# Folded inverses, post-norms behind the maxima, and output halves copied before they are squared, in a hybrid attention layer

## The chip, the cores and the metric

The kernel runs on one core of one Trainium2 chip. The metric is the device time of one execution in microseconds, taken as the median of several runs.

TensorE (PE in the profile) multiplies matrices into PSUM, VectorE (DVE), ScalarE (ACT) and GpSimd (POOL) work on rows of elements, and SyncE (SP) issues transfers. PEld is the loading of a matmul's weights.

## The reference

One layer of a streaming encoder, for a prompt of 2048 frames and for 32 new frames of a running stream with 1024 old ones:

```python
h = rmsnorm(x, g_pre)
u_a, gate_a, q, k, v, qi, ki, wi, gate_b = split(h @ w_in)
y_a = pool_mixer(u_a)                      # trailing means, a linear map per group
score = einsum(wi, relu(qi @ ki))          # 8 index heads of 32; only visible chunks of 64
sel = top_k(score, 256)                    # per query
logits = q @ k[sel] * HEAD_DIM**-0.5 + rel_bias[bucket(sel - pos)]   # 8 heads of 64, 2 kv heads
y_b = softmax(logits) @ v[sel]
mixed = concat([y_a * silu(gate_a), y_b * silu(gate_b)])
y = x + rmsnorm(mixed @ w_out, g_post)
```

## The kernel before

The queries are cut into 17 tiles: 16 of 128 prompt frames and one with the 32 new frames, tile 16. A first phase (not touched) projects, makes the pool branch and the index scores and leaves q, gates and scores in DRAM. The second phase, function `phase2`, runs through steps t = -1 to 19. A softmax over the selected keys is done as a softmax over all visible keys plus a mask of -1e30 on those that were not selected.

In step t, side by side:

- TensorE makes for each job (kv head, key tile) of tile t the logits (four matmuls, lines 1613 to 1618: high and low part of q, mask, and the row maximum taken away, "shift"), and two jobs later the weighted values (L1633, which sum the softmax's denominators in the same product). In between come the logits of tile t+1 that only serve its row maxima (L1599) and the output product of tile t-2 (L1648), in two halves of 512 columns with eight matmuls each, both into the one PSUM bank `wide[1][:, 0:512]`. A tile t below 16 has 2(t+1) jobs.
- ScalarE exponentiates each job into one of four buffers `E` (L1576), copies sums and denominators out of PSUM (L1515, L1517), takes the two output halves (kind "Y": square with an accumulated sum, L1564, then copy into `osb`, L1568), and makes the first 16 rounds of the search for the 256th score of tile t+3 (L1542 and small steps).
- VectorE makes rounds 16 to 25 of the search of tile t+2 (kind "R", L345 to L352) and its mask ("C", `set_mask`, L370 to L1693), the maxima of tile t+1 ("M", L1711), from them the shift ("S", L1716 and eight times L1721), the inverses of the denominators of tile t-1 ("I", L1727), and the post-norm of tile t-3 ("P", `post_norm`: a root by three Newton rounds on one column each, then L1736).
- GpSimd multiplies the exponentials of the six nearest key tiles of each kv head with the position bias (L1501), multiplies the sums of tile t-1 with the inverses and the gate (`mean`, L1460 and L1466, the result `yT` feeds the output product), and adds the residual to tile t-3 (`residual`, L1473).
- SP issues the loads of the next tiles and the store of tile t-3, in the order of its program; where it waits, all that is behind it waits.

The order on each engine is written out by `in_order`, which gives each kind of work a first and a last place within the step, between 0 and 1, and sorts. VectorE's today:

```python
return in_order((rounds, 0.0, 0.8), ([("M", *m) for m in maxima_of(t + 1)], 0.08, 0.78),
                ([("I", t - 1)] if 0 <= t - 1 < NT else [], 0.2, 0.2),
                ([("P", t - 3)] if 0 <= t - 3 < NT else [], 0.5, 0.5),
                ([("S", t + 1)] if 0 <= t + 1 < NT else [], 0.79, 0.79),
                ([("C", u)] if searched(u) else [], 0.9, 0.9))
```

Three PSUM banks hold the maxima's logits in turn, two hold the jobs' logits. Tiles from `FIRST` = 6 on are searched in phase 2. `NT` is 17, `ST` is 16, `NKV` 2, `HD` 64, `GRP` 4 and `P` 128.

Of the kernel before, what the change touches and what calls it, by code (L numbers as in the profile page):

```python
# [16 lines left out]
ALU = mybir.AluOpType  # L17
# [218 lines left out]
def build(nc, A):  # L236
    ctx = ExitStack()
    with ctx:
# [8 lines left out]
        def dram(name, shape, dt=F32):  # L247
# [10 lines left out]
        k_dram = dram("sample_keys_scratch", (NKV, P, PAST + P))  # L258

# [19 lines left out]
               ma_dram, s_dram, m_dram, g_dram, k_dram)  # L279
        phase2(nc, A, sb, sem, identf, identb, onesb, k2, home, loaded, unit, xs, first_q, banks, wide, q_dram, gb_dram,  # L280
               ma_dram, s_dram, m_dram, g_dram, k_dram)
# [127 lines left out]
def phase1(nc, A, sb, sem, identf, identb, onesb, k2, home, loaded, unit, xs, first_q, banks, wide, q_dram, gb_dram, ma_dram,  # L409
           s_dram, m_dram, g_dram, k_dram):  # L410
# [806 lines left out]
def phase2(nc, A, sb, sem, identf, identb, onesb, k2, home, loaded, unit, xs, first_q, banks, wide, q_dram, gb_dram, ma_dram,  # L1217
           s_dram, m_dram, g_dram, k_dram):
# [41 lines left out]
    HALVED = 1 + 3 * ZOOM_AT  # L1260

# [21 lines left out]

    def dve_step(t):
        u = t + 2
        rounds = [("R", u, r) for r in range(ZOOM_AT, ALL_ROUNDS)] if searched(u) else []
        return in_order((rounds, 0.0, 0.8), ([("M", *m) for m in maxima_of(t + 1)], 0.08, 0.78),
                        ([("I", t - 1)] if 0 <= t - 1 < NT else [], 0.2, 0.2),
                        ([("P", t - 3)] if 0 <= t - 3 < NT else [], 0.5, 0.5),
                        ([("S", t + 1)] if 0 <= t + 1 < NT else [], 0.79, 0.79),  # L1290
                        ([("C", u)] if searched(u) else [], 0.9, 0.9))

    def act_step(t):
        u = t + 3
        pieces = []
        if searched(u):
            pieces = [("N", u)]
            for r in range(ZOOM_AT):
                pieces += [("K", u, r), ("T", u, r)]
        return in_order(([("E", *j) for j in jobs(t)], 0.0, 1.0), (pieces, 0.02, 0.96),  # L1300
                        ([("Y", t - 2, 0)] if 0 <= t - 2 < NT else [], 0.5, 0.5),
                        ([("Y", t - 2, 1)] if 0 <= t - 2 < NT else [], 1.0, 1.0))

    with ExitStack() as st:
# [9 lines left out]

        act_junk = sb(st, "act_junk", [P, SEQ], BF16)
# [13 lines left out]
        sq = sb(st, "sq", [P, 512], BF16)  # L1329
        mxp = sb(st, "mxp", [P, NH, 4], F32)  # L1330
        nmax = sb(st, "nmax", [P, NH], F32)
        ss2 = sb(st, "ss2", [P, NT, 2], F32)
# [28 lines left out]
        sums_out, recip_done = sem("sums_out"), sem("recip_done")  # L1361
        mean_done, yT_done = sem("mean_done"), sem("yT_done")
        o_full, o_free = sem("o_full"), sem("o_free")
# [3 lines left out]
        with nc.Block() as block:  # L1367
            @block.sync
            def _(sp):
# [29 lines left out]

                def load_out_weights(i):  # L1400
# [3 lines left out]
                for t in range(NT + 3):  # L1404
# [20 lines left out]
                    if t + 4 >= FIRST + 3:  # L1425
                        load_S(t + 4)
                    if t >= 3:
# [26 lines left out]
            def _(pool):  # L1454
                def mean(t):

                    pool.wait_ge(recip_done, t + 1)
# [29 lines left out]
                for t in range(NT + 3):  # L1487
                    todo = jobs(t)
                    for i in range(len(todo) + 1):
                        if i == len(todo) // 3 and 0 <= t - 1 < NT:  # L1490
                            mean(t - 1)
                        if i == 2 * len(todo) // 3:
                            if t - 3 >= 0:
                                residual(t - 3)
# [11 lines left out]
            def _(act):  # L1506
# [20 lines left out]
                for t in range(NT + 2):  # L1527
                    for kind, *at in act_step(t):
# [30 lines left out]
                        elif kind == "Y":  # L1559
                            b, i = at  # L1560
                            act.wait_ge(o_full, 2 * b + i + 1)
                            if 2 * b + i:
# [265 lines left out]
```

## Time and profile before

| | before |
|---|---|
| median of 3 runs | 1710.84 us (1708.82 to 1711.71) |
| profiled execution | 1709.82 us |
| its span, first to last instruction | 1708.0 us |
| busy TensorE, VectorE, ScalarE, GpSimd | 1571.0, 1212.5, 893.6, 473.1 us |
| mean granted TensorE clock | 0.966 |

Phase 2 begins at about 800 us. Step 6 begins at 979.8 us, step 12 at 1333.4, step 13 at 1408.3, step 14 at 1485.9, step 15 at 1562.4 and step 16 at 1637.3, each taken as the start of the first logits matmul of its tile. Busy times of matmuls overlap with their neighbours' and their ends are modelled, so starts are the better measure of TensorE's pace.

### The profile page before, as it was taken

What the parts mean: (1) busy time and instruction counts of PE and PEld (TensorE: products, weight loads), DVE (VectorE), ACT (ScalarE), POOL (GpSimd) and SP (SyncE); (2) the same over time, 40 slices, a digit from 0 to 9 for tenths busy, and PEclk for the clock granted to TensorE, in tenths of its full rate; (3) what the DMA queues carried; (4) which work ended last, traced back from release to release, by engine and by line L of the source; (5) the groups of instructions that cost most, each with busy time, mean ns of one, the idle gap of its engine ahead of it and who ended that gap; (6) DMA issues with size and microseconds to landing.
All of it is one profiled execution on the core that took longest, in us unless ns stands there. A gap on an engine that the chain in (4) does not pass through costs nothing.

```text
span 1708.0 us, 17799 instructions
## 1 busy us (share of the span) xinstructions
PE 1571.0 (92%) x5191; PEld 877.6 (51%) x5191; DVE 1212.5 (71%) x2940; ACT 893.6 (52%) x1684; POOL 473.1 (28%) x384
## 2 busy tenths in 40 slices
PE   7999899989998989887888988999999999899996
PEld 4555555555555867655444444444444444455552
DVE  5412555557767878875549999999998999985422
ACT  3112333344434334452299988998888786523331
POOL 0112111121112112111344443433433333322241
PEclk9999999989999989988899999999999999999999
DMA  9312322221111110047533222220230211201001
GB/s 360 73 39 49 95 52 53 63 70 60 51 52 49 41 59 32 35 149 199 163 93 102 63 67 56 82 84 25 60 87 25 51 33 30 62 11 39 31 32 49
DMA packets 91978, 120.76 MB, mean 71 GB/s; under 512 B 17149, under 2 KB 63805, under 8 KB 91498
## 3 DMA queue, kind: packets, MB, share of 16 engines
q1 hardware_dynamic: 90506, 115.44, 21.7%
q10 hardware_dynamic: 1376, 4.19, 2.1%
q8 instruction: 42, 0.69, 0.2%
q14 instruction: 54, 0.44, 0.1%
HBM read 76.06 MB, written 43.54 MB: 70 GB/s over the span
## 4 chain that ended last, share of the span: by engine, by line
PE 23%; DVE 17%; ACT 6%; issue 5%; POOL 2%; POOLq 0%; DVEq 0%; ACTq 0%
PE wide L1648 7%; PE wide L1633 7%; DVE above L345 6%; DVE max_junk L1711 3%; ACT act_junk L1542 2%; PE bank L1613 2%; PE bank L1614 2%; PE bank L1615 2%; PE bank L1618 2%; POOL E L1501 1%; PE bank L1599 1%; DVE den L1727 1%; ACT E L1576 1%; DVE reach L383 1%; DVE S L379 1%
## 5 line engine op out<-in xcount | busy, mean ns | idle before, releaser
L931 PE MATMUL bank<-hT,home 128*128 128x512 f32 (+2 forms) x1280 | 489.5, 523 | 4.6 <-ACT kq L831 2.0
L1501 POOL TENSOR_TENSOR E<-E,home 128x512 f32<-128x512 f32 (+1 forms) x174 | 251.9, 1451 | 446.6 <-ACT E L1576 446.5
L931 PEld LDWEIGHTS bank<-hT,home 128*128 128x128 f32 x1280 | 241.2, 195 | 173.3 <-issue 150.6
L1633 PE MATMUL wide<-E,home 128*128 128x512 f32 x544 | 284.8, 605 | 9.9 <-POOL E L1501 9.7
L1576 ACT ACTIVATE E<-bank 128x512 f32<-128x512 f32 (+1 forms) x290 | 165.5, 571 | 244.9 <-PE bank L1618 243.2
L907 ACT ACTIVATE relu<-wide 128x1024 f32<-128x1024 f32 (+7 forms) x192 | 153.3, 802 | 173.5 <-PE wide L949 98.9
L1183 DVE SCALAR_TENSOR_TENSOR S<-relu,wi,S 128x1024 f32<-128x1024 f32 (+7 forms) x168 | 175.1, 1042 | 78.6 <-ACT relu L907 68.9
L1711 DVE CUSTOM_DVE_ANT_0 max_junk<-bank,mask 128x512 bf16<-128x512 f32 (+3 forms) x230 | 136.9, 614 | 68.9 <-PE bank L1599 55.4
L1648 PE MATMUL wide<-home 128*128 128x512 f32 x272 | 142.3, 614 | 23.2 <-ACT osb L1568 23.0
L949 PE MATMUL wide<-kiT,qiT 96*128 96x512 f32 (+3 forms) x304 | 136.4, 520 | 23.5 <-ACT relu L907 23.4
L1542 ACT ACTIVATE act_junk<-S,minus_cand 128x1152 bf16<-128x1152 f32 (+5 forms) x105 | 155.4, 1480 | 1.4
L931 PE MATMUL bank<-home,hT 128*128 128x296 f32 (+1 forms) x544 | 146.7, 410 | 2.5 <-ACT hT L815 2.5
L1648 PE MATMUL wide<-home,yT 128*128 128x512 f32 x272 | 135.8, 593 | 0.0
L1633 PEld LDWEIGHTS wide<-E,home 128*128 128x128 f32 x544 | 104.0, 194 | 55.5 <-POOL E L1501 17.7
L931 PEld LDWEIGHTS bank<-home,hT 128*128 128x128 f32 x544 | 106.5, 198 | 31.4 <-issue 4.6
L345 DVE TENSOR_SCALAR_CACHE_REDUCE above<-S,search 128x1152 bf16<-128x1152 f32 (+5 forms) x70 | 118.6, 1694 | 0.5
L744 POOL TENSOR_TENSOR win<-U 128x512 f32<-128x512 f32 (+11 forms) x20 | 20.1, 1005 | 356.8 <-ACT U L851 356.8
L1615 PE MATMUL bank<-identb,mask 128*128 128x512 bf16 (+1 forms) x290 | 112.8, 389 | 0.0
L1613 PE MATMUL bank<-first_q,k 128*128 128x512 f32 x182 | 107.5, 591 | 4.7 <-issue 2.6
L1618 PE MATMUL bank<-shift,onesb 128*128 128x512 bf16 (+1 forms) x290 | 109.6, 378 | 0.0
L1599 PE MATMUL bank<-k,first_q 128*128 128x512 f32 (+3 forms) x145 | 92.0, 659 | 14.5 <-DVE mxp L1711 9.7
L1711 DVE CUSTOM_DVE_ANT_0 max_junk<-wide,mask 128x512 bf16<-128x512 f32 (+3 forms) x114 | 65.3, 573 | 38.9 <-PE wide L1599 21.4
(204 smaller groups left out, 2390.0 us busy)
## 6 DMA issues: line engine op xcount, KB each, us to landing
xs<-x_prompt SPq DMA_DIRECT2D x16, 512.0 KB, 4.1
home<-w_in SPq DMA_DIRECT2D x16, 512.0 KB, 13.2
xr<-x_prompt SPq DMA_DIRECT2D x16, 512.0 KB, 4.3
y_prompt<-osb SPq DMA_DIRECT2D x16, 512.0 KB, 2.9
first_q<-q_high_scratch SPq DMA_DIRECT2D x24, 256.0 KB, 5.1
s_scratch<-S SPq DMA_DIRECT2D x11, 512.0 KB, 2.7
first_q<-q_low_scratch SPq DMA_DIRECT2D x18, 256.0 KB, 4.1
gb<-gb_scratch SPq DMA_DIRECT2D x17, 256.0 KB, 5.4
```

The lines of the kernel that those rows point to most:

```text
L345: dve.tensor_scalar((B.above, B.reach)[i][:, 0:s.shape[1]], s, B.cand[:, i:i + 1], None, ALU.is_ge, ALU.add, accum_out=B.cnt[:, i:i + 1]). ...
L907: act.activation(relu[:, k % 2, 0:b - a], wide[k % 2][:, 0:b - a], ACT.Relu)\
L931: mm = pe.matmul(out, stationary(c), moving(c), start=(c == 0), stop=(c == DC - 1))
L1183: dve.scalar_tensor_tensor(row, relu[:, k % 2, 0:b - a], w, row, ALU.mult, ALU.add)\
L1501: pool.tensor_tensor(E[:, k % 4, :, 0:n], E[:, k % 4, :, 0:n], EB[:, kv * GRP:(kv + 1) * GRP, off:off + n], ALU.mult)\
L1542: act.activation(act_junk[:, 0:w], S[sslot(u)][:, 0:w], ACT.Sign, bias=minus_cand[:, u % 2:u % 2 + 1], accum_out=act_sum[:])\
L1576: act.activation(E[:, k % 4, :, 0:n], banks[2 + k % 2][:, 0:GRP * n].rearrange("p (j n) -> p j n", j=GRP), ACT.Exp).then_inc(fl_free, 1)
L1615: pe.matmul(bank, mask[:, t % 3, kt * P:(kt + 1) * P], identb[:, 0:n].rearrange("p (a n) -> p a n", a=1).broadcast_to([P, GRP, n]), start= ...
L1618: pe.matmul(bank, onesb[:], shift[:, t % 2, kv * GRP:(kv + 1) * GRP, 0:n], start=False, stop=True)\
L1633: pe.matmul(wide[0][:, kv * 512:kv * 512 + GRP * n].rearrange("p (j n) -> p j n", j=GRP), values[:, kt, kv:kv + 2, :].rearrange("p a d -> ...
L1648: mm = pe.matmul(wide[1][:, 0:512], stat, wout[:, c, i * 512:(i + 1) * 512], start=(c == 0), stop=(c == DC - 1))
L1711: dve.tensor_tensor_reduce(junk[:, k % 2, 0:b - a], max_banks[k % 3][:, 0:b - a], mask[:, t % 3, a:b], 1.0, LEAST, ALU.add, ALU.max, mxp[: ...
```

## The change

Three things change. First, for tiles 5 to 14 (`FOLDED`) the denominators, 512 values in each of two partitions (copies in 64 partitions each), are folded by two transfers into 8 values on each of 128 partitions, inverted there, and brought back through DRAM with two broadcasting transfers; GpSimd's `mean` waits for these. VectorE's inverse moves from 0.2 to 0.4 of a step, `mean` from one third to two thirds of the jobs. Second, the post-norm moves behind the shift, from 0.5 to 0.80, in steps 6 to 15 (`long`), and the residual on GpSimd to the end of the step's jobs. Third, ScalarE only copies each output half (at 0.46 and 0.96 of the step), and squares both halves from `osb` in one instruction at 0.06 of the following step; TensorE waits for one count a half instead of two. Beside these, the shift of 8 heads is one VectorE instruction with broadcast operands.

```diff
+        r_dram = dram("reciprocal_scratch", (2, NKV, 1, GRP * P))
...
+    FOLDED = range(FIRST - 1, NPT - 1)
...
+    def long(t):
+
+        return FIRST <= t < ST
+
     def dve_step(t):
...
-                        ([("I", t - 1)] if 0 <= t - 1 < NT else [], 0.2, 0.2),
-                        ([("P", t - 3)] if 0 <= t - 3 < NT else [], 0.5, 0.5),
                         ([("S", t + 1)] if 0 <= t + 1 < NT else [], 0.79, 0.79),
+                        ([("I", t - 1)] if 0 <= t - 1 < NT else [], *((0.4, 0.4) if t - 1 in FOLDED else (0.2, 0.2))),
+                        ([("P", t - 3)] if 0 <= t - 3 < NT else [], *((0.80, 0.80) if long(t) else (0.5, 0.5))),
                         ([("C", u)] if searched(u) else [], 0.9, 0.9))
...
-                        ([("Y", t - 2, 0)] if 0 <= t - 2 < NT else [], 0.5, 0.5),
-                        ([("Y", t - 2, 1)] if 0 <= t - 2 < NT else [], 1.0, 1.0))
+                        ([("Y", t - 2, 0)] if 0 <= t - 2 < NT else [], 0.46, 0.46),
+                        ([("Y", t - 2, 1)] if 0 <= t - 2 < NT else [], 0.96, 0.96),
+                        ([("Z", t - 3)] if 0 <= t - 3 < NT else [], 0.06, 0.06))
...
+                def fold(t):
+
+                    i, turn = t % 2, t - FOLDED[0]
+                    sp.wait_ge(sums_out, 4 * (t + 1))
+                    for kv in range(NKV):
+                        sp.dma_start(folded[kv * HD:(kv + 1) * HD, i],
+                                     den[kv * HD:kv * HD + 1, i].rearrange("p (a n) -> p a n", a=HD))\
+                          .then_inc(folded_in[i], 16)
+                    sp.wait_ge(recip_done, t + 1)
+                    sp.dma_start(r_dram[i].rearrange("k o (a n) -> (k o a) n", a=HD), folded[:, i]).then_inc(folded_out, 16)
+                    sp.wait_ge(folded_out, 16 * (turn + 1))
+                    for kv in range(NKV):
+                        sp.dma_start(den[kv * HD:(kv + 1) * HD, i], r_dram[i, kv].broadcast_to([HD, GRP * P]))\
+                          .then_inc(spread_in, 16)
...
                     if t + 4 >= FIRST + 3:
                         load_S(t + 4)
+                    if t - 1 in FOLDED:
+                        fold(t - 1)
...
-                    pool.wait_ge(recip_done, t + 1)
+                    if t in FOLDED:
+                        pool.wait_ge(spread_in, 32 * (t - FOLDED[0] + 1))
+                    else:
+                        pool.wait_ge(recip_done, t + 1)
...
-                        if i == len(todo) // 3 and 0 <= t - 1 < NT:
+                        if i == (2 if t - 1 in FOLDED else 1) * len(todo) // 3 and 0 <= t - 1 < NT:
                             mean(t - 1)
-                        if i == 2 * len(todo) // 3:
-                            if t - 3 >= 0:
-                                residual(t - 3)
+                        if i == (len(todo) if long(t) else 2 * len(todo) // 3) and t - 3 >= 0:
+                            residual(t - 3)
...
-                            if 2 * b + i:
-                                act.wait_ge(o_free, 4 * b + 2 * i)
-                            act.activation(sq[:], wide[1][:, 0:512], ACT.Square,
-                                           accum_out=ss2[:, b, i:i + 1]).then_inc(o_free, 1)
                             if i == 0 and b >= 2:
                                 act.wait_ge(y_out[b % 2], 16 * (b // 2))
                             act.activation(osb[:, b % 2, i * 512:(i + 1) * 512], wide[1][:, 0:512], ACT.Copy).then_inc(o_free, 1)
+                        elif kind == "Z":
+                            b = at[0]
+                            act.wait_ge(o_free, 2 * b + 2)
+                            act.activation(sq[:], osb[:, b % 2], ACT.Square, accum_out=ss2[:, b:b + 1])\
+                               .then_inc(squared, 1)
...
-                    if c == 0 and 4 * t + 2 * i:
-                        pe.wait_ge(o_free, 4 * t + 2 * i)
+                    if c == 0 and 2 * t + i:
+                        pe.wait_ge(o_free, 2 * t + i)
...
-                    for h in range(NH):
-                        ins = dve.tensor_scalar(shift[:, t % 2, h, :], identb[:], nmax[:, h:h + 1], None, ALU.mult)
-                    ins.then_inc(shift_done, 1)
+                    dve.tensor_tensor(shift[:, t % 2], identb[:].rearrange("p (a n) -> p a n", a=1).broadcast_to([P, NH, P]),
+                                      nmax[:].rearrange("p (h n) -> p h n", n=1).broadcast_to([P, NH, P]), ALU.mult)\
+                       .then_inc(shift_done, 1)
 
                 def invert_sums(t):
+                    if t in FOLDED:
+                        dve.wait_ge(folded_in[t % 2], 32 * (1 + (t - FOLDED[0]) // 2))
+                        dve.reciprocal(folded[:, t % 2], folded[:, t % 2]).then_inc(recip_done, 1)
+                        return
...
-                    dve.wait_ge(o_free, 4 * (t + 1))
-                    link(dve.tensor_tensor(root[:, 3:4], ss2[:, t, 0:1], ss2[:, t, 1:2], ALU.add))
-                    dve.wait_ge(dk, n)
-                    n = inverse_root(dve, dk, n, root[:, 0:1], root[:, 1:2], root[:, 2:3], root[:, 3:4], 1.0 / D)
+                    dve.wait_ge(squared, t + 1)
+                    n = inverse_root(dve, dk, n, root[:, 0:1], root[:, 1:2], root[:, 2:3], ss2[:, t:t + 1], 1.0 / D)
```

## Rows read from the trace of the kernel before

**Rows 1.** Windows: length; busy PE, PEld, DVE, ACT, POOL (instructions); clock; DMA.

```profile
979.80:1485.90 506.10, 467.93 (x1475) 230.60 (x1473) 482.09 (x1038) 418.69 (x776) 192.66 (x120) 0.99 0.19 54
...
1333.40:1408.30 74.90, 68.54 (x223) 33.67 (x221) 72.02 (x143) 61.86 (x105) 26.63 (x16) 1.00 0.16 44
1562.40:1637.30 74.90, 74.90 (x249) 38.02 (x248) 21.84 (x71) 23.59 (x43) 20.41 (x16) 1.00 0.13 36
...
1395.20:1420.50 25.30, 22.67 (x72) 10.55 (x71) 24.78 (x33) 19.72 (x36) 14.20 (x6) 1.00 0.27 62
...
1347.20:1395.20 48.00, 45.47 (x152) 23.26 (x152) 45.64 (x111) 38.65 (x66) 12.54 (x9) 1.00 0.06 23
```

**Rows 2.** Timeline of TensorE late in step 15: start, us, instruction.

```profile
1626.81 0.79 PE L1613 MATMUL bank<-first_q,k 128*128 128x512 f32 x1
...
1629.43 0.80 PE L1613 MATMUL bank<-first_q,k 128*128 128x512 f32 x1
...
1631.20 0.79 PE L1613 MATMUL bank<-first_q,k 128*128 128x512 f32 x1
```

**Rows 3.** TensorE's waits in steps 6 to 13: us in total, times, longest.

```profile
PE bank L1599 <- DVE mxp L1711: 16.5, 15, 2.6
PE wide L1633 <- POOL E L1501: 8.1, 8, 1.7
```

**Rows 4.** Groups of VectorE by form, steps 6 to 13: busy us, mean ns.

```profile
L1727 DVE RECIPROCAL den<-den 128x512 f32<-128x512 f32 x8 | 26.8, 3347 | 0.0
...
L1721 DVE TENSOR_SCALAR shift<-identb,nmax 128x128 bf16<-128x128 bf16 x64 | 18.1, 354 | 0.7 <-DVE nmax L1716 0.5
```

**Rows 5.** The tile of the denominators: shortest, median and longest reciprocal in ns.

```profile
L1727 DVE RECIPROCAL den<-den x17: 953/3348/3354, 816.1 to 1666.5; 128x512 f32<-128x512 f32 x16, 128x128 f32<-128x128 f32 x1
```

**Rows 6.** Timeline of VectorE, the post-norm in step 12.

```profile
1376.27 0.15 DVE L1732 TENSOR_TENSOR root<-ss 128x1 f32<-128x1 f32 x1
1376.46 0.15 DVE L286 TENSOR_SCALAR root<-root 128x1 f32<-128x1 f32 x1
...
1378.58 1.28 DVE L1736 SCALAR_TENSOR_TENSOR osb<-osb,root,gpost 128x1024 f32<-128x1024 f32 x1
```

**Rows 7.** Timeline of SP's queue in step 12.

```profile
1340.54 0.33 SPq L1376 DMA_DIRECT2D S<-s_scratch  x1
1382.41 0.34 SPq L1431 DMA_DIRECT2D y_prompt<-osb  x1
```

**Rows 8.** DMA issues of phase 2: count, KB each, median us to landing.

```profile
gb<-gb_scratch SPq DMA_DIRECT2D x16, 256.0 KB, 5.4
...
gpost<-g_post SPq DMA_DIRECT2D x1, 512.0 KB, 16.3
...
y_sample<-osb SPq DMA_DIRECT2D x1, 128.0 KB, 1.9
```

**Rows 9.** Timeline of VectorE, the post-norm in step 16.

```profile
1645.75 0.35 DVE L1732 TENSOR_TENSOR root<-ss 128x1 f32<-128x1 f32 x1
...
1647.57 1.20 DVE L296 SCALAR_TENSOR_TENSOR root<-root 128x1 f32<-128x1 f32 x1
...
1651.06 1.29 DVE L1736 SCALAR_TENSOR_TENSOR osb<-osb,root,gpost 128x1024 f32<-128x1024 f32 x1
```

**Rows 10.** Timelines of GpSimd and VectorE at the end of step 12.

```profile
1398.21 1.28 POOL L1501 TENSOR_TENSOR E<-E,home 128x512 f32<-128x512 f32 x1 [1.15 <-ACT E L1576]
1401.33 11.63 POOL L1501 TENSOR_TENSOR E<-E,home 128x512 f32<-128x512 f32 x4 [1.84 <-ACT E L1576]
...
1401.54 5.07 DVE L379 TENSOR_TENSOR_SCAN S<-reach,above 128x1920 f32<-128x1920 bf16 x1
```

**Rows 11.** Timeline of ScalarE, the last output half.

```profile
1698.40 0.60 ACT L1564 ACTIVATE sq<-wide 128x512 bf16<-128x512 f32 x1 [7.22 <-PE wide L1648]
...
1698.99 0.59 ACT L1568 ACTIVATE osb<-wide 128x512 f32<-128x512 f32 x1
```

**Rows 12.** TensorE's waits for output halves: steps 2 to 5, step 16 onwards.

```profile
PE wide L1648 <- ACT osb L1568: 12.7, 6, 3.3
...
PE wide L1648 <- ACT osb L1568: 5.0, 4, 1.4
```

More of the change, by code:

```diff
@@ L278, in build @@
         phase1(nc, A, sb, sem, identf, identb, onesb, k2, home, loaded, unit, xs, first_q, banks, wide, q_dram, gb_dram,
-               ma_dram, s_dram, m_dram, g_dram, k_dram)
+               ma_dram, s_dram, m_dram, g_dram, k_dram, r_dram)
         phase2(nc, A, sb, sem, identf, identb, onesb, k2, home, loaded, unit, xs, first_q, banks, wide, q_dram, gb_dram,
-               ma_dram, s_dram, m_dram, g_dram, k_dram)
+               ma_dram, s_dram, m_dram, g_dram, k_dram, r_dram)
 def inverse_root(dve, done, n, ms, y, tmp, ss, scale):
@@ L409, in phase1 @@
 def phase1(nc, A, sb, sem, identf, identb, onesb, k2, home, loaded, unit, xs, first_q, banks, wide, q_dram, gb_dram, ma_dram,
-           s_dram, m_dram, g_dram, k_dram):
+           s_dram, m_dram, g_dram, k_dram, r_dram):
     steps, inside = phase1_steps()
@@ L1217, in phase2 @@
 def phase2(nc, A, sb, sem, identf, identb, onesb, k2, home, loaded, unit, xs, first_q, banks, wide, q_dram, gb_dram, ma_dram,
-           s_dram, m_dram, g_dram, k_dram):
+           s_dram, m_dram, g_dram, k_dram, r_dram):
     def chunks(t):
@@ L1313, in phase2 @@
         mask = sb(st, "mask", [P, 3, SEQ], BF16)
+        sq = sb(st, "sq", [P, D], BF16)
         act_junk = sb(st, "act_junk", [P, SEQ], BF16)
@@ L1328, in phase2 @@
         yT = sb(st, "yT", [P, 2, 4, P], F32)
-        sq = sb(st, "sq", [P, 512], BF16)
+        folded = sb(st, "folded", [P, 2, NH], F32)
         mxp = sb(st, "mxp", [P, NH, 4], F32)
         nmax = sb(st, "nmax", [P, NH], F32)
-        ss2 = sb(st, "ss2", [P, NT, 2], F32)
+        ss2 = sb(st, "ss2", [P, NT], F32)
         root = sb(st, "root", [P, 4], F32)
@@ L1361, in phase2 @@
         sums_out, recip_done = sem("sums_out"), sem("recip_done")
+        folded_in = [sem(f"folded_in{i}") for i in range(2)]
+        folded_out, spread_in = sem("folded_out"), sem("spread_in")
         mean_done, yT_done = sem("mean_done"), sem("yT_done")
-        o_full, o_free = sem("o_full"), sem("o_free")
+        o_full, o_free, squared = sem("o_full"), sem("o_free"), sem("squared")
         post_done = sem("post_done")
@@ L1526, in _ @@
                 waiting = []
-                for t in range(NT + 2):
+                for t in range(NT + 3):
                     for kind, *at in act_step(t):
```

## Prediction

> **What bounds the kernel now.** I read the windows by step first. A step here is one turn t of phase 2's loop: logits, exponentials and weighted values of tile t, the maxima of tile t+1, the output product of tile t-2. Steps 6 to 13 took 506.1 us; VectorE was busy for 482.1 of them, TensorE for 468 [rows 1]. Both look full, so I asked next what TensorE would need alone. In step 15, where it waits for nothing, a job with an output product beside it takes 2.62 us from one first logits matmul to the next, a job alone 1.77 [rows 2]; so an output product is 0.85 and one 512-column pass about (1.77 - 0.85) / 4 = 0.23. Step 15 then needs 32 x 1.77 + 16 x 0.85 + 18 x 0.23 = 74.4 us against 74.9 measured [rows 1]: the reckoning holds. Steps 6 to 13 have 168 jobs, 128 output products and maxima worth 184 passes: 297.4 + 108.8 + 42.3 = 448.5 us. So they run 58 us above TensorE's own work and only 24 above VectorE's. The waits say the same: TensorE's longest is for the maxima's two banks, 16.5 us, the next for GpSimd's bias products, 8.1 [rows 3]. VectorE sets these eight steps; step 15 and most of step 14 belong to TensorE.
>
> VectorE's step has two halves. Between the last maximum of tile 13 and the first of tile 14 lie shift, mask and the first search rounds, 25.3 us without a maximum; TensorE was busy for 22.7 of them with work that needs no maxima. In the stretch of tile 13's maxima, 48.0 us, VectorE was busy for 45.6 [rows 1]. TensorE's own work there is some 42 us: the maxima go from 0.15 (three buffers filled) to 0.76 of its step, so 0.61 of 26 jobs, 9.5 output products and 25 passes. The second half is where VectorE holds the step up by itself.
>
> **Folded inverses.** Eight full reciprocals in steps 6 to 13 take 3.35 us each [rows 4]. The folded one has 8 elements a partition. The two shapes seen, 3348 ns for 512 and 953 for 128 [rows 5], give 6.24 ns an element and 0.20 us at 8. Bounds: 0.15, a one-column operation [rows 6], and 0.95. I take 0.20: 3.15 saved, 25.2 us over eight steps. In step 14 and 15 the saving falls where TensorE is full and counts nothing.
>
> The price is five transfers a tile on SP's queue: two fold, one goes out, two spread. Behind them on SP stand the store, the load of the residual's input and the next step's loads. Today SP stands from the score load at 1340.5 to the store at 1382.4 with nothing to do [rows 7], so the fold uses idle time. The fold's rows are issued behind the step's loads, 7 us into step 12 today [rows 7]; with the store before them pushed by some 10 us and landings of 5.4, they are there near 20, and the inverse is asked for later: VectorE begins step 12's maxima at 1347.2, 13.8 us in [rows 1], 0.18 of the step where 0.08 is written, so place 0.4 comes near 0.5, plus 3 us of post-norm: 27 us in a step 6 of 49.
>
> After it come the way out and the spread. Transfers land in 1.9 us at best, in a burst in 5.4, the slowest seen in 16.3 [rows 8]. I take 2 + 2.5 + 1 us of issuing, 5.5, because nothing else is queued then; bounds 4 and 33. GpSimd multiplies at two thirds of the jobs, in front of most of the second head group's bias products. In step 6 the mean is done at 27 + 5.5 + 2 x 1.28 = 35 us; the weighted values of the job behind it run two jobs late, at 11/14 of 49 = 38.5. So it costs nothing, and the room after the inverse is 38.5 - 27 - 2.6 = 9 us in step 6 and 62 - 38.5 - 2.6 = 21 in a step 12 of 71.
>
> **Shift in one instruction.** Eight small ones take 18.1 / 8 = 2.26 us a step; a two-source operation on 1024 elements takes 1.28 [rows 4, 6]. It can wait for one GpSimd product (1.28) first [rows 10]. Bounds 1.28 and 2.56; I take 1.7, the row and a third of such a wait: 0.56 saved, 4.5 us.
>
> **Post-norm after the shift.** The sum of the two halves goes (0.19, start to start [rows 6]): 1.5 us. The other 12 instructions stay, but the place changes. Today GpSimd stands idle waiting for exactly this chain, which takes 1376.27 to 1379.86, 3.59 us [rows 6]. In step 16, beside GpSimd's products, the same chain took 1645.75 to 1652.35, 6.60 us [rows 9]. The new place, 0.8 of a step, lies among the second group's bias products. Bounds: 0 and 3.0 us more a step; I take 1.0, nearer to the quiet row since the products leave gaps, so -8.0 us. The chain moves 3.4 us out of the maxima's stretch into the other half, which was level with TensorE; that half becomes longer, but VectorE's sum decides both.
>
> The Trainium skill (SBUF — State Buffer, section "SBUF: two separate sides") calls this an exclusive lock: a VectorE operation with two SBUF inputs and a GpSimd operation exclude each other for the whole instruction. The rows agree: GpSimd's four products of 1.28 took 11.63 us while VectorE ran the scan and the two-source operations behind it [rows 10]. Applied to every small operation of the chain, this rule would give the upper bound, 3.0 in place of 1.0, and 16 us less gain.
>
> In return the residual no longer stands on GpSimd in front of bias products, and the mask's operations slide past the step's last products. TensorE's waits there are 8.1 us [rows 3]; I take 3 of them. What is late next is the residual: it ends some 10 us into the following step and the store follows, before the copy at 0.46 wants that buffer.
>
> **Copy first, square later.** Square to copy, start to start, is 0.59 us [rows 11]; TensorE waits for the pair. Steps 2 to 5 have six such waits, 12.7 us, the end four, 5.0 us [rows 12]. In steps 2 to 5 I take 6 x 0.59 less a little for ScalarE, itself near full with the search: 3 us. The waits in steps 6 to 13 bring nothing while VectorE binds. At the end three waits in line save 1.8; the last square, now 1024 wide (estimate 1.2 from two of 0.6, and 0.2 to read the sum), stands after the copy and gives back 0.6: 1.2 us.
>
> **Sum.** 25.2 + 4.5 + 1.5 - 8.0 + 3 = 26.2 us in steps 6 to 13, 3 in 2 to 5, 1.2 at the end: 30.4. The profiled execution took 1709.8 us (1.8 around its span); 1679.4. The median of the runs is 1.0 above it: 1680.
>
> **Rivals.** *TensorE's pace.* If shorter VectorE stretches also end its own idle 24 us, steps 6 to 13 come near VectorE's 459 (TensorE's 448.5 lies below): 47 + 4 = 51 us off, 1660. For it: GpSimd's jam by the scan, in most steps, is the start of VectorE's idle; against: the two engines then stand within 3% and interleave in a fixed order. Chance 0.14.
>
> *The first half becomes the brake.* The post-norm lengthens the stretch without maxima to about 28 to 31 us while TensorE has 23 to 25 of work; the maxima's stretch can fall no further than TensorE's 42, 6.0 less than today. With a chain of 6.6 us a step gives up 6.0 (less the shift's 0.6) and gains 6.0 to 6.7: eight steps bring some 5, the rest 4: 1702. For it rows 9, against it that VectorE's own sum still falls. Chance 0.15.
>
> *The inverses come too late* (slower). GpSimd then stands in front of the second group's bias products, and TensorE's weighted values behind them. The room is 9 us in step 6 and about 2 more in each following step. A way out at the slowest landing and a spread at a burst's, 16.3 + 5.4 + 1 = 22.7 us, would cost 14, 12, 10 ... 2 us in steps 6 to 12, 56 in all: 1736. It outweighs the 30 from about 19 us on. Against: the quiet queue; the 16.3 comes from a full 512 KB broadcast to all partitions in the burst of step 1. Chance 0.10.
>
> *Nothing measurable:* the gains are what VectorE then spends waiting, 1711. Against: rows 3. Chance 0.05.
>
> **Numbers.** The forecast, own range 1665 to 1693, has 0.56. A measurement tells about 0.2% (3.4 us) from no change. Faster: 0.56 + 0.14 + 0.14 of the third case = 0.84; same 0.06; slower 0.10. To hold 8 in 10 the range takes in the forecast, most of the third case and two thirds of the first rival: 1657 to 1705.
>
> **What would show it.** Steps 6 to 13 at 475 to 485 us; a folded reciprocal near 0.2; one shift of 1.3 to 2.6; the chain of the post-norm at 3.4 to 6.4; TensorE's waits for maxima cut to a third, but moved to the first maxima of a step; GpSimd not waiting for the spread in front of bias products; waits for the copied halves down by 0.6 each. Wrong if VectorE's busy time falls by 25 us and the steps don't, or if GpSimd's wait for the spread shows up in TensorE.

## The result, and the profile after

| | before | after |
|---|---|---|
| median | 1710.84 us (5 runs, 1708.82 to 1714.02) | 1719.69 us (5 runs, 1718.05 to 1720.34) |
| ratio, 95% interval | | 1.0049 (1.0034 to 1.0063) |
| profiled execution, span | 1708.0 us | 1717.9 us |
| busy TensorE, VectorE | 1571.0, 1212.5 us | 1573.6, 1191.8 us |
| mean granted TensorE clock | 0.966 | 0.957 |

The changed kernel is slower by 0.5%, where 1.8% faster was forecast. Step 6 now begins at 975.8 us, step 12 at 1335.9, step 13 at 1413.8, step 14 at 1492.4, step 15 at 1574.4 and step 16 at 1649.5. The windows of the changed kernel, columns as in [rows 1]: steps 6 to 13, step 14, the stretch without maxima between tiles 13 and 14, and the stretch of tile 13's maxima:

```profile
975.80:1492.40 516.60, 470.43 (x1475) 237.55 (x1473) 465.76 (x967) 415.53 (x758) 192.37 (x119) 0.96 0.20 55
1492.40:1574.40 82.00, 76.40 (x247) 39.16 (x245) 65.23 (x138) 22.30 (x39) 26.45 (x15) 0.96 0.14 36
...
1402.40:1431.70 29.30, 24.34 (x77) 11.45 (x75) 28.39 (x39) 21.91 (x39) 15.31 (x7) 1.00 0.32 83
1354.40:1402.40 48.00, 47.24 (x152) 24.75 (x152) 39.81 (x98) 38.09 (x64) 10.26 (x8) 0.93 0.05 18
```

Against [rows 1], VectorE's busy time in steps 6 to 13 fell by 16.3 us (482.1 to 465.8), and these steps took 10.5 us more (506.1 to 516.6). The stretch without maxima grew from 25.3 to 29.3 us. The stretch of tile 13's maxima is 48.0 us as before, although VectorE has only 39.8 us of work in it instead of 45.6. What it saved there it now spends waiting; its waits in steps 6 to 13, of the changed kernel:

```profile
DVE max_junk L1741 <- PE bank L1629: 22.4, 25, 2.1
DVE max_junk L1741 <- PE wide L1629: 16.3, 16, 2.5
```

38.7 us, where VectorE had waited 11.4 us in the same places before:

```profile
DVE max_junk L1711 <- PE bank L1599: 7.8, 10, 2.1
DVE max_junk L1711 <- PE wide L1599: 3.6, 5, 1.5
```

And TensorE, same steps, to be set against [rows 3] (the matmul of the maxima is now L1629, VectorE's maximum L1741, the weighted values L1663):

```profile
PE bank L1629 <- DVE mxp L1741: 30.1, 6, 5.9
PE wide L1629 <- DVE mxp L1741: 9.3, 3, 8.3
PE wide L1663 <- POOL E L1530: 5.5, 4, 1.7
```

[rows 3] show the waits for the maxima's two banks only; the third buffer, a half of `wide[1]`, has a line of its own, before:

```profile
PE wide L1599 <- DVE mxp L1711: 7.8, 6, 2.7
```

So 21 waits of at most 2.7 us, 24.3 us in all, have become nine, 39.4 us in all. Seven of these nine are long (4.0 to 8.3 us), one a step from step 7 on. Each of the seven stands in front of the fourth matmul of a tile's maxima: three buffers are filled, and the first is not read yet. The longest, in TensorE's timeline of step 12:

```profile
1345.17 0.79 PE L1629 MATMUL bank<-k,first_q 128*128 128x512 f32 x1
1345.80 1.02 PE L1678 MATMUL wide<-home 128*128 128x512 f32 x2
...
1355.16 0.58 PE L1629 MATMUL wide<-k,first_q 128*128 128x256 f32 x1 [8.34 <-DVE mxp L1741]
```

What VectorE did meanwhile (its timeline: the shift, the post-norm from its first to its last instruction, the scan of the mask, the end of the second search round, the first maximum):

```profile
1326.50 1.23 DVE L1750 TENSOR_TENSOR shift<-identb,nmax 128x1024 bf16<-128x1024 bf16 x1
1327.64 0.15 DVE L287 TENSOR_SCALAR root<-ss 128x1 f32<-128x1 f32 x1
...
1329.49 1.14 DVE L297 SCALAR_TENSOR_TENSOR root<-root 128x1 f32<-128x1 f32 x1
...
1331.44 1.28 DVE L1768 SCALAR_TENSOR_TENSOR osb<-osb,root,gpost 128x1024 f32<-128x1024 f32 x1
...
1337.01 4.77 DVE L380 TENSOR_TENSOR_SCAN S<-reach,above 128x1792 f32<-128x1792 bf16 x1
...
1354.25 0.16 DVE L353 SCALAR_TENSOR_TENSOR search<-search,search 128x1 f32<-128x1 f32 x1
1354.40 0.69 DVE L1741 CUSTOM_DVE_ANT_0 max_junk<-wide,mask 128x512 bf16<-128x512 f32 x1
```

The post-norm took 5.08 us here (1327.64 to 1332.72), in front of mask and search and so in front of the first maximum. The last reading is the clock. A window around that stand:

```profile
1350.90:1361.10 10.20, 5.94 (x12) 3.07 (x13) 9.35 (x24) 3.17 (x5) 0.00 (x0) 0.50 0.55 140
```

The granted clock is 0.50, the 1.2 GHz level, for 10.2 us from within the stand to behind it. Such a stretch lies beside each of the seven; in steps 6 to 13 the trace's clock records add up to 44.4 us at 0.50, against 10.2 before. Not all of that is lost, since a part of it lies within the stands, when TensorE had nothing to do: by the windows of these stretches it worked for 31.6 of the 44.4 us (5.94 of the 10.2 above), and before for all of the 10.2. Half of the additional 21.4 us of work, some 11 us, is an estimate of what the clock took on top of the stands' own length.

### The profile page after: what moved, and what is told of

The parts are those of the page before. It is cut to its first block, busy times and chain, and to the rows that moved or that the text cites. A ratio compares the mean times of both kernels' runs of the same rounds, so it can differ in the third digit from the quotient of the medians.

```text
span 1717.9 us, 17661 instructions
## 1 busy us (share of the span) xinstructions
PE 1573.6 (92%) x5191; PEld 885.1 (52%) x5191; DVE 1191.8 (69%) x2804; ACT 890.1 (52%) x1650; POOL 478.6 (28%) x384
## 3 DMA queue, kind: packets, MB, share of 16 engines
q1 hardware_dynamic: 95146, 118.15, 22.4%
## 4 chain that ended last, share of the span: by engine, by line
PE 28%; DVE 16%; ACT 5%; issue 4%; POOL 1%; POOLq 0%; ACTq 0%; DVEq 0%
PE wide L1663 8%; PE wide L1678 8%; DVE above L346 4%; PE bank L1643 2%; PE bank L1644 2%; PE bank L1645 2%; PE bank L1629 2%; PE bank L1648 2%; ACT act_junk L1571 2%; DVE reach L384 1%; DVE max_junk L1741 1%; DVE above L381 1%; PE wide L1629 1%; DVE S L380 1%; DVE home L380 1%
## 5 line engine op out<-in xcount | busy, mean ns | idle before, releaser
L1530 POOL TENSOR_TENSOR E<-E,home 128x512 f32<-128x512 f32 (+1 forms) x174 | 243.3, 1401 | 509.5 <-ACT E L1606 509.5
L1663 PE MATMUL wide<-E,home 128*128 128x512 f32 x544 | 286.4, 609 | 5.8 <-POOL E L1530 5.7
L1741 DVE CUSTOM_DVE_ANT_0 max_junk<-bank,mask 128x512 bf16<-128x512 f32 (+3 forms) x230 | 137.5, 616 | 90.3 <-PE bank L1629 85.5
L1678 PE MATMUL wide<-home 128*128 128x512 f32 x272 | 141.2, 610 | 10.1 <-ACT osb L1593 10.0
L1663 PEld LDWEIGHTS wide<-E,home 128*128 128x128 f32 x544 | 106.3, 197 | 50.4 <-POOL E L1530 10.1
L1629 PE MATMUL bank<-k,first_q 128*128 128x512 f32 (+3 forms) x145 | 95.4, 685 | 26.0 <-DVE mxp L1741 21.5
L1741 DVE CUSTOM_DVE_ANT_0 max_junk<-wide,mask 128x512 bf16<-128x512 f32 (+3 forms) x114 | 65.6, 575 | 49.9 <-PE wide L1629 45.9
```

Of the source, the lines that this page charges most:

```text
L1530: pool.tensor_tensor(E[:, k % 4, :, 0:n], E[:, k % 4, :, 0:n], EB[:, kv * GRP:(kv + 1) * GRP, off:off + n], ALU.mult)\
L1629: pe.matmul(max_banks[k % 3][:, 0:b - a], qh[t % 3][:, kv, j, :], keys[:, a:b], start=True, stop=True)\
L1663: pe.matmul(wide[0][:, kv * 512:kv * 512 + GRP * n].rearrange("p (j n) -> p j n", j=GRP), values[:, kt, kv:kv + 2, :].rearrange("p a d -> ...
L1678: mm = pe.matmul(wide[1][:, 0:512], stat, wout[:, c, i * 512:(i + 1) * 512], start=(c == 0), stop=(c == DC - 1))
L1741: dve.tensor_tensor_reduce(junk[:, k % 2, 0:b - a], max_banks[k % 3][:, 0:b - a], mask[:, t % 3, a:b], 1.0, LEAST, ALU.add, ALU.max, mxp[: ...
```

## The experiments

Times are medians, ratios are to the kernel before on the same chip (1709.3 to 1710.4 us), with the 95% interval. Two runs are compared by their medians even where their chips differ, since the kernel before varies by less than 2 us between these. "Halved" is the time at a granted clock of 0.50 in steps 6 to 13.

**The post-norm back in its place, all else kept.**

```diff
-  ([("P", t - 3)] ..., *((0.80, 0.80) if long(t) else (0.5, 0.5))),
+  ([("P", t - 3)] ..., 0.5, 0.5),
...
-  if i == (len(todo) if long(t) else 2 * len(todo) // 3) and t - 3 >= 0:
+  if i == 2 * len(todo) // 3 and t - 3 >= 0:
```

> The changed kernel with the post-norm back at 0.5 of a step and the residual back at two thirds of the jobs; folded inverses, one-instruction shift and copy-first stay. Theory A (the post-norm in the stretch without maxima makes TensorE stand at the first maxima of each step, and its granted clock falls after each such stand): the stretch without maxima returns from 22.6-29.3 to 17-25 us, the halved clock in phase 2 shrinks to the few pieces of before, and the time falls by about the 30 us of the prediction's other terms, to 1680 (1670 to 1692). Theory B (the fold's transfers, or the late mean, hold the steps up): it stays at 1712 to 1722, because the fold is untouched. Theory C (copying first, with the late square, costs): 1712 to 1722 as well.

1700.19 us, 0.9942 (0.9927 to 0.9957): 19.5 us faster than the changed kernel. The move is what made the change a loss. But the time lies in no theory's range: theory A had the direction and expected 1670 to 1692. What held the rest back is taken up below (post-norm back and no fold). Post-norm and residual were moved together here, as in the change, since the residual waits for the post-norm.

**The post-norm's move alone**, in the kernel before.

```diff
-  ([("P", t - 3)] ..., 0.5, 0.5),
   ([("S", t + 1)] ..., 0.79, 0.79),
+  ([("P", t - 3)] ..., *((0.80, 0.80) if FIRST <= t < ST else (0.5, 0.5))),
...
-  if i == 2 * len(todo) // 3:
+  if i == (len(todo) if FIRST <= t < ST else 2 * len(todo) // 3):
```

> The kernel before with nothing but the post-norm moved to 0.80 and the residual to the end of the jobs in steps 6 to 15. Theory A: the stretch without maxima grows by about 5 us, TensorE stands 4 to 8 us in one piece in each of nine steps and runs some 7 us at the lower clock behind it; the maxima's stretch keeps its full reciprocal, so little is given back: 1720 to 1745. Theories B and C: nothing of the fold or the copies is here, so the time is 1705 to 1714 or lower.

1740.01 us, 1.0173 (1.0155 to 1.0191), 30 us slower, with 44.4 us halved, as in the changed kernel. TensorE's waits for the maxima:

```profile
PE bank L1599 <- DVE mxp L1711: 36.3, 7, 8.1
PE wide L1599 <- DVE mxp L1711: 11.6, 3, 8.3
```

The move alone is the loss; the other edits pay part of it back.

**The changed kernel without the fold.**

```diff
-  FOLDED = range(FIRST - 1, NPT - 1)
+  FOLDED = range(0)
```

> The changed kernel without the fold: full reciprocals at 0.2, the mean at one third of the jobs, no extra transfers; the moved post-norm stays. Theory A: VectorE stands idle 4 to 7 us in each stretch of maxima of the changed kernel, so 3.15 us more work there costs little: 1719 to 1730. Theory B: the time falls below the kernel before, to 1690 to 1708.

1724.3 us, 1.0081 (1.0065 to 1.0098). In the changed kernel the fold was worth 4.6 us of the 25.2 forecast: VectorE's shorter inverse lies in the stretch where VectorE waits.

**The maxima later on TensorE.** VectorE's order is untouched; TensorE does more of the other work before its first maxima.

```diff
-  ([("M", *m) for m in maxima_of(t + 1)], 0.08, 0.78),     # pe_step
+  ([("M", *m) for m in maxima_of(t + 1)], 0.18 if long(t) else 0.08, 0.78),
```

> The changed kernel with one number other: in steps 6 to 15 TensorE's maxima begin at 0.18 of its step in place of 0.08, so that some 5 us more of its other work stand in front of the first maxima. Theory A: the single long stand at the first maxima mostly goes, and with it the fall of the clock; 1680 to 1698 with the post-norm still in its new place. If only the post-norm's longer duration beside GpSimd's products costs (5.1 in place of 3.6 us): 1715 to 1722, as the order of TensorE's work does not shorten it.

1680.01 us, 0.9823 (0.9806 to 0.9839): 39.7 us off the changed kernel by one number. Halved fell to 10.2 us, and the longest stand to 3.8:

```profile
PE bank L1629 <- DVE mxp L1741: 14.9, 5, 3.8
PE wide L1629 <- DVE mxp L1741: 3.2, 4, 1.7
```

The residual still stands at the end of the jobs here, so its move is not by itself what made the changed kernel slow.

**Idle passes in the stand.** 22 logits matmuls, whose results the next job overwrites, stand in front of the fourth maxima matmul in steps 7 to 14, so that TensorE works where it stood. They add 8 x 22 passes of work. (The expectation says steps 7 to 15; the edit acts in 7 to 14.)

```diff
+    FILLS = 22
...
+  if FIRST < t < NPT - 1 and fx[tuple(at)] == fx[t + 1, 0, 0] + 3:
+      fill(next(a for k, *a in step[place:] if k == "A"))
...
+  def fill(job):
...
+      for _ in range(FILLS):
+          pe.matmul(banks[2 + k % 2][:]..., k2[kv][...], qh[t % 3][:, kv], start=True, stop=True)
```

> The changed kernel with 22 more logits passes in steps 7 to 15, put in front of the fourth maxima matmul of each, the one at which TensorE stands 4 to 8 us; they write the PSUM bank of the next job, which that job's own first matmul overwrites, so the outputs stay and TensorE has 5 us of idle work in place of the stand. Theory A1 (the stand costs its length and then again a half of each stretch at the lower granted clock): the clock stays high and the time falls although work was added, to 1692 to 1710. Theory A2 (the stand's length is the whole cost and the clock falls in stretches that cost nothing): 1716 to 1730.

1704.35 us, 0.9973 (0.9961 to 0.9985). TensorE's waits for the maxima in this run:

```profile
PE wide L1630 <- DVE mxp L1753: 4.1, 2, 3.3
...
PE bank L1630 <- DVE mxp L1753: 1.0, 3, 0.4
```

With more work the kernel is 15.3 us faster, and halved falls from 44.4 to 6.8. In the profiled pair 13.6 us of this lie in steps 6 to 14 (11.6 and 2.0); the other 1.7 lie before step 2, where the edit changes nothing. The passes are no shorter than the waits that they replace: in steps 7 to 13 they add 7 x 22 x 0.23 = 35.4 us (0.23 a pass, the prediction's estimate), and the waits for the maxima fell by 34.3, from 39.4 to 5.1. So the 13.6 us are put down to the clock. The estimate of above gives about the same: in steps 6 to 14 TensorE worked for 35.6 us at 0.50 in the changed kernel and for 5.8 here, and half of the difference is 15. The rest of the loss stays, since the idle passes fill the stand without using it.

**The later maxima without the post-norm's move**: in the kernel before, and with the post-norm back in the changed one (the edits of above, combined).

```diff
-  ([("M", *m) for m in maxima_of(t + 1)], 0.08, 0.78),     # pe_step
+  ([("M", *m) for m in maxima_of(t + 1)], 0.18 if FIRST <= t < ST else 0.08, 0.78),
```

> The kernel before with nothing but TensorE's maxima from 0.18 in place of 0.08 in steps 6 to 15. Theory A (the later start helps because the post-norm has moved in front of it): here VectorE's stretch without maxima is level with TensorE's work already and the stretch of the maxima holds the full reciprocal and the post-norm, so nothing is gained: 1705 to 1728. Rival (the later start is a gain of its own, whatever stands on VectorE): 1680 to 1698.

1715.64 us, 1.0045 (1.0029 to 1.0061).

> The changed kernel with the post-norm and the residual back at their old places and TensorE's maxima from 0.18 in steps 6 to 15. Theory A (the two halves have to be level, post-norm in the first half with a later start, or in the second with the early one): VectorE then has the post-norm among maxima that are asked for in less time, so it is no better than the post-norm back alone, 1697 to 1712. Rival (the post-norm's new place never helps, only the later start does): below 1680.

1706.31 us, 0.9979 (0.9967 to 0.999). Without the post-norm's move the later start makes things worse by 6 us in both kernels. It is no gain of its own; it is worth 40 us only to a kernel whose VectorE comes late.

**Post-norm back and no fold**: the kernel before with the shift in one instruction and the copied halves.

```diff
-  FOLDED = range(FIRST - 1, NPT - 1)
+  FOLDED = range(0)
...
-  ([("P", t - 3)] ..., *((0.80, 0.80) if long(t) else (0.5, 0.5))),
+  ([("P", t - 3)] ..., 0.5, 0.5),
```

(and the residual at two thirds)

> The changed kernel with the post-norm and the residual at their old places and no fold: what is left of the change is the one-instruction shift and copying first. The prediction's terms for these two are 4.5 + 1.5 + 3 + 1.2 us, which gives 1700; with the post-norm back and the fold it was 1700.2, so if the fold is worth its 25 us there, this run is at 1720 to 1730, and if the fold's saving falls into waits, at 1698 to 1710.

1693.35 us, 0.9905 (0.9891 to 0.992), 16.5 us faster, and below both ranges of the expectation. So with the post-norm at 0.5 the fold costs 6.8 us (1700.19). In the run with the fold GpSimd's two products of the mean wait for the inverse and then fall upon the post-norm; GpSimd and VectorE there:

```profile
1368.67 1.28 POOL L1490 TENSOR_TENSOR osum<-osum,den 128x512 f32<-128x512 f32 x1 [2.42 <-DMA den<-reciprocal_scratch]
1370.12 1.27 POOL L1496 TENSOR_TENSOR yT<-osum,gb 128x512 f32<-128x512 f32 x1 [0.17 <-POOL osum L1490]
```

```profile
1368.77 1.20 DVE L294 TENSOR_TENSOR root<-root 128x1 f32<-128x1 f32 x1
1370.00 0.16 DVE L297 SCALAR_TENSOR_TENSOR root<-root 128x1 f32<-128x1 f32 x1
1370.19 1.22 DVE L300 SCALAR_TENSOR_TENSOR root<-root 128x1 f32<-128x1 f32 x1
```

Two operations on one column take 1.2 us instead of 0.16, about as long as the product beside them, and the chain of 3.4 us takes 5.5 in five of the eight steps. Without the fold it ran in 3.40 us in seven of the eight steps. The next two runs try this reading.

**Post-norm at 0.42**, behind the folded inverse, while GpSimd still waits.

```diff
-  *((0.80, 0.80) if long(t) else (0.5, 0.5))
+  *((0.42, 0.42) if long(t) else (0.5, 0.5))
```

(with the residual back at two thirds, as in the first experiment)

> The changed kernel with the residual back at two thirds of the jobs and the post-norm at 0.42 of the step, just behind the folded inverse, while GpSimd still waits for the inverse to come back (at 0.50 the same kernel gave 1700.2, without the fold 1693.4). Theory of the collision: the post-norm runs beside an idle GpSimd, takes 3.4 to 3.6 us instead of 5.5, and the folded inverse is no longer harmful: 1685 to 1694. Rival: what costs is the fold's transfers or the later mean, not the collision: 1699 to 1703 as at 0.50.

1708.5 us, 0.9995 (0.9982 to 1.0009): missed. The chain met one product, took 4.4 us in most steps instead of 5.5, and the time is 8 us worse. VectorE's timeline shows why:

```profile
1361.77 2.21 DVE L346 TENSOR_SCALAR_CACHE_REDUCE above<-S,search 128x1920 bf16<-128x1920 f32 x1
...
1365.09 0.19 DVE L1757 RECIPROCAL folded<-folded 128x8 f32<-128x8 f32 x1
1365.20 0.37 DVE L1741 CUSTOM_DVE_ANT_0 max_junk<-wide,mask 128x256 bf16<-128x256 f32 x1
...
1369.91 0.68 DVE L1741 CUSTOM_DVE_ANT_0 max_junk<-bank,mask 128x512 bf16<-128x512 f32 x1
```

A search round, the inverse, a single short maximum and the post-norm stand in line from 1361.77 to 1369.91, 8.1 us with one maximum; TensorE's next matmul of the maxima waited 4.32 us for it. By this reading not the chain's own length counts but the longest stretch with hardly a maximum in it, of whatever it is made.

**Post-norm at 0.60**, behind the mean's products and further from a round.

```diff
-  *((0.80, 0.80) if long(t) else (0.5, 0.5))
+  *((0.60, 0.60) if long(t) else (0.5, 0.5))
```

(and the residual at two thirds)

> The changed kernel with the residual back at two thirds of the jobs and the post-norm at 0.60 of the step, behind the mean's products (at 0.50, beside them, 1700.2; at 0.42, close behind a round of the search, 1708.5; without the fold at 0.50 1693.4). Theory: what costs is the longest stretch of VectorE with one maximum in it at most, which the mean's products beside the post-norm lengthen; at 0.60 the chain is back at 3.4 us, TensorE's stands over 3 us are gone, and the fold's shorter inverse is gained: 1680 to 1693. Rival: the fold itself costs (its landings, the later mean), wherever the post-norm stands: 1699 or more.

1679.73 us, 0.9824 (0.9808 to 0.984): 13.6 us better than the same without the fold at 0.50, 20.5 better than with it at 0.50. The chain is 3.40 to 3.66 us in six of the eight steps. TensorE's waits for the maxima in its steps 6 to 13:

```profile
PE bank L1629 <- DVE mxp L1741: 9.0, 7, 3.3
PE wide L1629 <- DVE mxp L1741: 2.1, 2, 1.3
```

11.1 us, where the same with the post-norm at 0.50 had 28.1 (22.4 and 5.7). So a kernel with the fold need not lose by it as at 0.50. How much of the 13.6 us is the fold's and how much the place's, and whether the fold gains at all at 0.60, stays open: 0.60 without the fold was not run.

**The shift alone**, in the kernel before.

```diff
-  for h in range(NH):
-      ins = dve.tensor_scalar(shift[:, t % 2, h, :], identb[:], nmax[:, h:h + 1], None, ALU.mult)
-  ins.then_inc(shift_done, 1)
+  dve.tensor_tensor(shift[:, t % 2], identb[:]...broadcast_to([P, NH, P]),
+                    nmax[:]...broadcast_to([P, NH, P]), ALU.mult).then_inc(shift_done, 1)
```

> The kernel before with the shift in one instruction and nothing else. By the prediction's term: 8 x 0.56 = 4.5 us less, 1705. Theory that the shift is worth more than VectorE's time for it, since it lies in the stretch without maxima and takes the shared port from GpSimd for a shorter time: 10 us or more, 1700 or less. Rival: the 17 us of shift and copied halves together are those of the copied halves: 1708 to 1711.

1697.99 us, 0.9945 (0.9929 to 0.9961), 11.4 us faster where 4.5 had been reckoned; the copied halves, with the sum of the two halves that goes with them, then have 1697.99 - 1693.35 = 4.6. The shift itself took 1.88 us on average here, near the 1.7 taken. In the profiled pair steps 6 to 13 fell by 7.8 us, 4.1 of them in step 6, where the granted clock rose from 0.97 to 1.00. That is 3.4 us at 0.50 less, which can be worth 1.7 us at most; the rest of step 6's gain is not explained. The other 3.7 us lie in seven steps, 0.5 a step as reckoned. The remaining 3.7 us lie before step 6, 1.5 of them in steps 2 to 5 and 2.2 before step 2; they are not explained either, and the start of step 2 varies from 824.0 to 827.9 us among all the profiled runs.

**The later maxima without the fold** (the two edits of above on the changed kernel).

```diff
+  FOLDED = range(0)
...
+  ([("M", *m) for m in maxima_of(t + 1)], 0.18 if long(t) else 0.08, 0.78),
```

> The changed kernel with TensorE's maxima from 0.18 of a step and without the fold (full inverses at 0.2). Theory: with the later maxima the stand of TensorE at the fourth maxima matmul is small, and the stretch of the maxima, in which the full inverse lies, sets the step again; then all of the 3.15 us a step comes back: 1680.0 + 8 x 3.15 = 1705. Rival: the fold is worth as little as with the early maxima, 1724.3 - 1719.7 = 4.6 us, since VectorE has idle time left there: 1685.

1703.44 us, 0.9974 (0.9963 to 0.9985). With the maxima at 0.18 the fold is worth 23.4 us, five times what it is worth at 0.08, and close to the 25.2 of the prediction. In part this closeness is luck: without the fold 27.2 us are halved, with it 10.2, and by the estimate of above (TensorE worked for 23.8 and 10.1 us of these) some 7 of the 23.4 us are the clock's.

**The maxima from 0.24, and from 0.30.**

```diff
+  ([("M", *m) for m in maxima_of(t + 1)], 0.24 if long(t) else 0.08, 0.78),
```

> The changed kernel with TensorE's maxima from 0.24 of a step (0.18 gave 1680.0, 0.08 gave 1719.7). Theory of the stretch without maxima: at 0.18 TensorE still stands for 1.6 to 3.8 us once a step and its clock is halved for 41.8 us of phase 2; a start at 0.24 takes most of that away, 1670 to 1678. Rival: at 0.24 the first maxima reach VectorE late, VectorE stands in front of its first one instead, and the maxima then run into the end of the step: 1685 or more.

1671.44 us, 0.9792 (0.9775 to 0.9808): the best version, 2.1% below the kernel before. Its windows (steps 6 to 13, the stretch of tile 13's maxima, the stretch without maxima behind it) and TensorE's waits:

```profile
976.20:1452.90 476.70, 460.68 (x1448) 229.00 (x1473) 454.57 (x967) 415.04 (x758) 179.21 (x119) 1.00 0.21 59
...
1326.70:1367.00 40.30, 38.30 (x128) 19.93 (x129) 38.48 (x98) 32.47 (x56) 10.28 (x8) 1.00 0.07 21
1367.00:1397.40 30.40, 28.21 (x89) 13.38 (x88) 28.71 (x38) 23.89 (x44) 16.08 (x7) 1.00 0.33 86
```

```profile
PE bank L1629 <- DVE mxp L1741: 6.1, 11, 1.2
...
PE wide L1629 <- DVE mxp L1741: 2.3, 5, 1.0
```

The stretch without maxima is even longer than in the changed kernel (30.4 us), but TensorE has 28.2 us of work for it, no wait for a maximum is over 1.2 us, and the clock is at 1.00 throughout these steps. Now the stretch of the maxima can shrink: 40.3 us instead of 48.0.

```diff
+  ([("M", *m) for m in maxima_of(t + 1)], 0.30 if long(t) else 0.08, 0.78),
```

> The changed kernel with TensorE's maxima from 0.30 of a step (0.08: 1719.7, 0.18: 1680.0, 0.24: 1671.4). Theory: at 0.24 VectorE already stands 0.8 to 1.0 us in front of the first maximum in the two longest steps; 0.06 of a step of 45 to 75 us is 2.7 to 4.5 us, so at 0.30 it stands 1 to 5 us in most steps and must make it up in the stretch of the maxima: 1675 to 1690. Rival: TensorE alone sets the time by now, and the place doesn't matter: 1668 to 1673.

1678.97 us, 0.982 (0.9803 to 0.9836). Beyond the optimum: VectorE waits for its first maximum, up to 4.0 us in steps 6 to 13 (in step 6) and 5.4 in step 14.

**The maxima from 0.24 with the post-norm at 0.60** and the residual at two thirds.

```diff
+  ([("M", *m) for m in maxima_of(t + 1)], 0.24 if long(t) else 0.08, 0.78),
...
+  ([("P", t - 3)] ..., *((0.60, 0.60) if long(t) else (0.5, 0.5))),
```

> TensorE's maxima from 0.24, as in the run that gave 1671.4, but with the post-norm at 0.60 and the residual at two thirds of the jobs. Theory of the balance: with the post-norm among the maxima the stretch without them is some 5 us shorter than TensorE's work up to 0.24, so VectorE waits for its first maximum and has more to do behind it: 1695 to 1710, near the 1706.3 of the same with 0.18 and 0.50. Rival: the later start alone brings the gain and the post-norm's place is indifferent then: 1668 to 1680.

1705.49 us, 0.9973 (0.9961 to 0.9986). With the maxima from 0.24 the move from 0.60 to 0.80 gains 34.1 us; with the maxima from 0.08 it costs 40.0 (1679.7 to 1719.7). VectorE's first maximum in step 13 of this run:

```profile
1420.12 0.69 DVE L1741 CUSTOM_DVE_ANT_0 max_junk<-bank,mask 128x512 bf16<-128x512 f32 x1 [7.15 <-PE bank L1629]
```

The place of the post-norm (with the fold; the residual at two thirds in the first two lines, at the end in the third) against the start of TensorE's maxima, in us:

| post-norm at | maxima from 0.08 | 0.18 | 0.24 | 0.30 |
|---|---|---|---|---|
| 0.50 | 1700.2 | 1706.3 | | |
| 0.60 | 1679.7 | | 1705.5 | |
| 0.80 (the change) | 1719.7 | 1680.0 | 1671.4 | 1679.0 |

## Why the prediction was wrong

**The step that failed** is "that half becomes longer, but VectorE's sum decides both". VectorE's sum is spent across two stretches, and TensorE can run only three maxima ahead of it. In the stretch without maxima TensorE had 22.7 us of work for 25.3 us [rows 1]; lengthening that by 4 us made TensorE stand, and what VectorE saved in the other stretch it could not use, because TensorE's maxima there are spread among its jobs at TensorE's own pace: TensorE was busy for 47.2 of the 48.0 us. Steps 6 to 13 took 10.5 us more where the prediction's sum had 26.2 less. The two stretches don't add up to one sum; each has its own limit. The table shows it from both sides: the same VectorE program gives 1671 or 1720 us, depending on TensorE's place for the maxima alone.

**The rival "the first half becomes the brake" named the place and the lengths** (28 to 31 us against the 29.3 measured behind tile 13) but came out at 1702. It missed the clock. TensorE's stand was one of 4 to 8 us a step instead of several of at most 2.7, and the clock fell to 1.2 GHz beside each: some 14 us by the idle passes. With these, 1702 becomes 1716, against 1719.7 measured. It also gave the stretch of the maxima 6.0 to 6.7 us of gain, while the profile shows none in tile 13's.

**Folded inverses, 25.2 us.** The instruction was sized rightly: 0.196 us against 0.20. The tile of the folded sums, changed kernel:

```profile
L1757 DVE RECIPROCAL folded<-folded x10: 189/196/197, 998.3 to 1605.2; 128x8 f32<-128x8 f32 x10
...
DMA to landing us min/median/max: 1.4/6.0/8.2
```

Where it was spent decided what it was worth: 4.6 us in the changed kernel, a loss of 6.8 with the post-norm at 0.50, 23.4 with the maxima from 0.18. "The inverses come too late" is out: the mean waits for the way back, but TensorE's waits for GpSimd fell from 8.1 to 5.5 us [rows 3], near the 3 us taken for them. In steps 7 to 14 the mean began 4.8 to 5.9 us after the inverse, where 5.5 had been taken. GpSimd's wait, steps 6 to 13:

```profile
POOL osum L1490 <- DMA den<-reciprocal_scratch: 17.3, 7, 4.1
```

**Post-norm, 1.0 us longer each.** It took 5.1 to 5.5 us, 5.21 on average, where 3.40 + 1.0 = 4.4 was taken (3.40 is the 3.59 of [rows 6] without the sum). In step 12, whose timeline stands above, two of its operations on one column took 0.86 and 1.14 us instead of 0.16, which is the whole of the 5.08 - 3.40 = 1.68 us, and they ended, at 1328.87 and 1330.63, within 0.02 us of the end of a product on GpSimd:

```profile
1327.14 1.72 POOL L1530 TENSOR_TENSOR E<-E,home 128x512 f32<-128x512 f32 x1 [1.73 <-ACT E L1606]
1329.31 1.30 POOL L1530 TENSOR_TENSOR E<-E,home 128x512 f32<-128x512 f32 x1 [0.46 <-ACT E L1606]
```

The exclusive lock of the Trainium skill (SBUF — State Buffer, section "SBUF: two separate sides") agrees with these two operations. As an upper bound for the whole chain, 3.0 us more, it was too high, since the rest of the chain ran between the products. This error is 6.5 us over eight steps; the wrong sign doesn't come from it.

**Copy first.** TensorE's waits for the halves in steps 2 to 5, and from step 16 on, changed kernel, against [rows 12]:

```profile
PE wide L1678 <- ACT osb L1593: 6.7, 3, 3.2
...
PE wide L1678 <- ACT osb L1593: 2.2, 3, 0.8
```

Steps 2 to 5 took 2.9 us less (3 forecast), the end 2.3 less (1.2 forecast). But 1.5 of the 2.9 us came with the shift alone, so 1.4 are the copies' own, although the waits for the halves fell by 6.0. The pair of runs with and without gives 4.6 for all of it, where 3 + 1.2 and the 1.5 of the sum make 5.7: right in size, not in its parts. **Shift:** VectorE's time was about right, the 11.4 us of the run not, as told above.

**Sum.** Of the 9.9 us by which the profiled span grew, steps 6 to 13 have 10.5 and step 14, counted as TensorE's own, 5.5 more (82.0 against 76.5), with a stand of 5.6 us and 6.8 us of halved clock; steps 2 to 5 and the end give 5.2 back, and about 1 us less lies before step 2. "Wrong if VectorE's busy time falls by 25 us and the steps don't" is what came, with 16 in place of 25.

## What to carry to other kernels

Where two engines hand over through a few buffers, draw up the sum not by step but by stretch: for the longest stretch in which the consumer takes nothing, compare its length with the work that the producer has for that time. Moving work into that stretch pays only if the producer's order is moved with it; here one number in TensorE's order made 1671 us out of 1720 (0.24 in place of 0.08), and raising the same number to 0.18 cost 6 us in the kernel before. And price one long stand of TensorE, of 4 to 8 us as here, above its length, since the granted clock fell beside each of them.

## What was not expected of the hardware

Short waits of TensorE for the maxima, 24.3 us in 21 with none over 2.7, left all but 10.2 us of steps 6 to 13 at full clock; one wait of 4 to 8 us a step went with 3.4 to 10.2 us at 0.50, and matmuls without use in its place made the kernel 15 us faster. A reciprocal of 8 elements a partition takes 0.196 us, so the 6.24 ns an element found from 128 and 512 [rows 5] holds down to very few, with about 0.15 us for the rest.
